# Hybrid decoder step: gate rows through DRAM, key norms on ScalarE, head steps one projection step earlier

## The reference, cut to what matters

```
q = l2_normalize(q) * DK_B ** -0.5 ; k = l2_normalize(k)       # over the 128 channels of a token
gcum = cumsum(g)                                               # over the tokens of a chunk
decay = where(tril, exp(gcum[:, None] - gcum[None, :]), 0)
lower = tril((k * beta) @ k.T * decay, -1)                     # solve (lower + I) u = ...
attn = (q @ k.T) * decay
kg = k * exp(gcum[-1] - gcum)
...
o = rms_norm(o, norm_g) * silu(z)
```

## Time and profile before

| | before |
|---|---|
| median of 3 runs | 2000.53 us (1999.17 to 2001.12) |
| the profiled execution: its own time, its span | 2001.81 us, 2000.0 us |
| PE busy, share of the span | 1962.6 us, 98% |
| DVE, ACT, POOL busy | 1234.6, 733.6, 670.3 us |
| chain that ended last, PE's share | 86% |

### The profile page before, as it was taken

How to read it: one execution, slowest core, us unless ns; L and a number is a source line. 1 busy time by engine, 2 the same in 40 slices (tenths; PEclk the granted TensorE clock), 3 DMA queues, 4 the chain that set the end, 5 groups by cost and what they waited for, 6 DMA issues and landing times.

```text
span 2000.0 us, 37378 instructions
## 1 busy us (share of the span) xinstructions
PE 1962.6 (98%) x15596; PEld 1902.4 (95%) x15596; DVE 1234.6 (62%) x2460; ACT 733.6 (37%) x1268; POOL 670.3 (34%) x659
## 2 busy tenths in 40 slices
PE   6999999999999999999999999999999999999997
PEld 4999999999999988889999999999999999999997
DVE  6666566756663435665433389999999954563334
ACT  5422222232222124544212255555555543352220
POOL 4123212311320222002211158888888840031110
PEclk9999999999999999999999999999999999999998
DMA  5221222112222234112344333333332322223333
GB/s 195 75 64 56 65 66 64 65 56 64 66 70 89 94 139 162 54 54 77 121 132 132 108 107 91 89 95 95 96 95 87 86 75 85 85 91 120 101 105 113
DMA packets 79721, 184.14 MB, mean 92 GB/s; under 512 B 26776, under 2 KB 35928, under 8 KB 79304
## 3 DMA queue, kind: packets, MB, share of 16 engines
q1 hardware_dynamic: 72304, 166.22, 27.2%
q0 software_dynamic: 3504, 9.63, 1.4%
q10 hardware_dynamic: 3744, 5.90, 0.8%
HBM read 162.66 MB, written 19.06 MB: 91 GB/s over the span
## 4 chain that ended last, share of the span: by engine, by line
PE 86%; DVE 10%; issue 1%; POOL 1%; ACT 1%; DMA 0%; SPq 0%; POOLq 0%; DVEq 0%; ACTq 0%
PE acc L580 71%; DVE arena L1551 2%; DVE full L1554 2%; PE acc L654 2%; DVE w_lo L1551 2%; PE gp L778 1%; DVE act_lo L1551 1%; PE acc L682 1%; POOL small L2295 1%; PE gp L788 1%; PE gp L884 1%; PE gp L770 1%; PE gp L936 1%; DVE full L1551 1%; PE gp L766 1%
## 5 line engine op out<-in xcount | busy, mean ns | idle before, releaser
L580 PE MATMUL acc<-act_hi,w_hi 128*128 128x288 f32 x3904 | 861.2, 302 | 0.3 <-DVE w_lo L1551 0.3
L580 PE MATMUL acc<-act_hi,w_lo 128*128 128x288 f32 x3904 | 836.4, 296 | 0.0
L580 PE MATMUL acc<-act_lo,w_hi 128*128 128x288 f32 x3904 | 835.4, 296 | 0.0
L580 PEld LDWEIGHTS acc<-act_hi,w_hi 128*128 128x128 f32 x3904 | 625.2, 189 | 14.7 <-issue 9.5
L580 PEld LDWEIGHTS acc<-act_hi,w_lo 128*128 128x128 f32 x3904 | 628.9, 189 | 0.0
L580 PEld LDWEIGHTS acc<-act_lo,w_hi 128*128 128x128 f32 x3904 | 627.9, 189 | 0.0
L2295 POOL TENSOR_TENSOR arena<-arena 128x512 f32<-128x512 f32 (+2 forms) x281 | 386.9, 1377 | 348.0 <-ACT arena L1397 284.1
L1093 ACT ACTIVATE w_hi<-w_raw 128x1024 fp32r<-128x1024 f32 x264 | 277.1, 1054 | 416.0 <-PE acc L580 309.9
L1551 DVE TENSOR_TENSOR w_lo<-w_raw,w_hi 128x1024 fp32r<-128x1024 f32 x264 | 382.4, 1468 | 41.3 <-ACT w_hi L1093 40.4
L1554 DVE SCALAR_TENSOR_TENSOR gp<-arena,par,gp 128x64 f32<-128x64 f32 (+1 forms) x688 | 248.0, 441 | 0.0
L1093 ACT ACTIVATE arena<-arena,par 128x512 f32<-128x512 f32 x240 | 165.1, 720 | 95.6 <-POOL arena L2295 88.0
(11 more groups left out here) (263 smaller groups left out, 1784.0 us busy)
## 6 DMA issues: line engine op xcount, KB each, us to landing
w_raw<-wt SPq DMA_DIRECT2D x264, 512.0 KB, 4.0
full<-x SPq DMA_DIRECT2D x16, 288.0 KB, 6.9
arena<-x SPq DMA_DIRECT2D x16, 288.0 KB, 3.7
arena<-x_scratch SPq DMA_DIRECT2D x16, 288.0 KB, 2.8
x_scratch<-full ACTq DMA_DIRECT2D x14, 288.0 KB, 3.9
out_y<-full SPq DMA_DIRECT2D x24, 144.0 KB, 1.9
arena<-state_in SPq DMA_DIRECT2D x6, 512.0 KB, 4.1
out_sdn<-arena POOLq DMA_DIRECT2D x6, 512.0 KB, 3.1
```

The costliest lines, as they stand in the source:

```text
L580: ins = pe.matmul(acc[:, s, i, 0:HALF], w[:, s, wk], a[:, k, i * HALF:(i + 1) * HALF], start=(k == 0 and j == 0), stop=(k == KT - 1 and j ...
```

## The change

What it does:

- The running sums of the gates of all heads come out of four more matmuls in `gate_sums`, once, with the 8 heads as output rows. DVE copies them to SBUF (`g_turned`), POOL stores them in DRAM (`g_dram`, 8 rows of 512), and for each head POOL loads one row into all 128 partitions (`gate_row`, `g_row`): for head 0 at step 30 of the unit before, for head `it + 1` at step 9 of the unit of head `it`. `gcum` and `gB` are gone; `dmask` reads `g_row` from SBUF and waits for that DMA.
- `sq` squares q alone. The squares of k are made by ACT from the transposed k in PSUM, four activations of 128 columns with a sum each (`ksq`), after `kv_tok`. `norm` has four matmuls in place of eight; `ssum` has two instructions and also waits for `ksq`.
- With `gcum` gone, `norm`, `gram` and all head steps behind them up to `so3`, with what the other engines do for them, stand one projection step earlier: `a3` at step 10, `so3` at step 28, `osq` and `f1` to `f5` at 29, `on` at 30. `o_chan` stays behind step 0. On DVE `kg` moves from step 1 to behind `attn`.

```
-PE_HEAD = (["kv_tok", "gcum", "norm", "gram"] + ...
+PE_HEAD = (["kv_tok", "norm", "gram"] + ...
-PE_PLAN = {1: "kv_tok", 2: "gcum", 3: "norm", 4: "gram"}
-PE_PLAN |= {11 + i: n for i, n in enumerate(PE_HEAD[4:-1])}
+PE_PLAN = {1: "kv_tok", 2: "norm", 3: "gram"}
+PE_PLAN |= {10 + i: n for i, n in enumerate(PE_HEAD[3:-1])}
-DVE_PLAN = {1: ["kg"], 2: ["dmask"], 3: ["ssum"], 4: ["vs", "Mt", "attn"], 6: ["mc", "solve", "Xt", "X"]}
+DVE_PLAN = {2: ["dmask", "ssum"], 3: ["vs", "Mt", "attn", "kg"], 5: ["mc", "solve", "Xt", "X"]}
-POOL_PLAN = {0: ["scalars", "gB"], 3: ["nrm", "rn", "bn", "bp"], 4: ["B"], 7: ["L3"], 8: ["L4"]}
+POOL_PLAN = {0: ["scalars"], 2: ["nrm", "rn", "bn", "bp"], 3: ["B"], 6: ["L3"], 7: ["L4"]}
...
                 pe.matmul(gp[:, 1, 80:144], ones[0:NS, :], gmask.rearrange("p h b -> p (h b)"), start=True, stop=True)
+                for c in range(NC):
+                    pe.matmul(gp[0:H, 2, c * P:(c + 1) * P], gates[:, :, KG, c], tri, start=True, stop=True)
...
-                elif name == "gcum":
-                    pe.wait_ge(pool_h.sem, pool_h.at("gB", it))
-                    for c in range(NC):
-                        ins = pe.matmul(gp[:, 2, ck(c)], gB[:, c, :], tri, start=True, stop=True)
                 elif name == "norm":
                     pe.wait_ge(act_h.sem, act_h.at("sq", it))
-                    for c in range(8):
-                        ins = pe.matmul(gp[:, 3, c:c + 1], sqkq_c[:, c, :], ones[:, 0:1], start=True, stop=True)
+                    for c in range(NC):
+                        ins = pe.matmul(gp[:, 3, c:c + 1], q_sq[:, ck(c)], ones[:, 0:1], start=True, stop=True)
...
+                elif name == "ksq":
+                    act.wait_ge(pe_h.sem, pe_h.at("kv_tok", it))
+                    for c in range(NC):
+                        ins = act.activation(k_sq[:, c, :], gp[:, 0, c * P:(c + 1) * P], ACT.Square,
+                                             accum_out=ksum[:, c:c + 1])
...
                 elif name == "dmask":
-                    pe_at("gcum")
-                    ins = tt(dec, bank4(2), per_group(negm, 4), ADD)
+                    dve.wait_ge(g_in, 16 * (it + 1))
+                    ins = tt(dec, g_row, per_group(negm, 4), ADD)
...
+            def gate_row(it):
+
+                row = g_dram[it].unsqueeze(0).to_broadcast([P, SEQ])
+                pool.dma_start(g_row, row.rearrange("p (c t) -> p c t", t=P)).then_inc(g_in, 16)
...
+                            if 8 * ti + e == 9 and it < H - 1:
+                                pool.wait_ge(dve_h.sem, dve_h.at("dmask", it))
+                                gate_row(it + 1)
+                        if hp == 0 and (ti, e) == (3, 2):
+                            pool.wait_ge(prep, 3)
+                            pool.dma_start(g_dram, g_turned).then_inc(g_stored, 16)
+                        if hp == 0 and (ti, e) == (3, 6):
+                            pool.wait_ge(g_stored, 16)
+                            gate_row(0)
```

More of the change, by code:

```diff
@@ L100 @@
 LV = range(FIRST, LEVELS)
-PE_HEAD = (["kv_tok", "gcum", "norm", "gram"] + [f"{s}{i}" for i in LV for s in ("a", "x")]
+PE_HEAD = (["kv_tok", "norm", "gram"] + [f"{s}{i}" for i in LV for s in ("a", "x")]
            + ["u0", "so0"] + [f"{s}{c}" for c in range(1, NC) for s in ("s", "u", "so")] + ["o_chan"])
@@ L104 @@
 assert LEVELS == 7
-DVE_HEAD = (["kg", "dmask", "ssum", "vs", "Mt", "attn", "mc", "solve", "Xt", "X"]
+DVE_HEAD = (["dmask", "ssum", "vs", "Mt", "attn", "kg", "mc", "solve", "Xt", "X"]
             + [n for i in LV for n in [f"X{i}"] + [f"T{i}"] * (i in IN_BLOCKS)]
@@ L108 @@
             + ["on", "y"])
-ACT_HEAD = ["sq", "decay"] + [f"A{i}" for i in LV] + [f"q{c}" for c in range(1, NC)] + ["osq"]
-POOL_HEAD = (["scalars", "gB", "nrm", "rn", "bn", "bp", "B"] + [f"L{i}" for i in LV]
+ACT_HEAD = ["sq", "ksq", "decay"] + [f"A{i}" for i in LV] + [f"q{c}" for c in range(1, NC)] + ["osq"]
+POOL_HEAD = (["scalars", "nrm", "rn", "bn", "bp", "B"] + [f"L{i}" for i in LV]
              + ["f1", "f2", "f3", "f4", "f5"])
-PE_PLAN = {1: "kv_tok", 2: "gcum", 3: "norm", 4: "gram"}
-PE_PLAN |= {11 + i: n for i, n in enumerate(PE_HEAD[4:-1])}
+PE_PLAN = {1: "kv_tok", 2: "norm", 3: "gram"}
+PE_PLAN |= {10 + i: n for i, n in enumerate(PE_HEAD[3:-1])}
 def counts(names):
@@ L145 @@
 PE_AT = {n: i for i, n in PE_PLAN.items()}
-ACT_PLAN = {1: ["sq"], 2: ["decay"]} | {PE_AT[f"a{i}"]: [f"A{i}"] for i in LV}
-ACT_PLAN |= {PE_AT[f"s{c}"]: [f"q{c}"] for c in range(1, NC)} | {30: ["osq"]}
-DVE_PLAN = {1: ["kg"], 2: ["dmask"], 3: ["ssum"], 4: ["vs", "Mt", "attn"], 6: ["mc", "solve", "Xt", "X"]}
+ACT_PLAN = {1: ["sq", "ksq"], 2: ["decay"]} | {PE_AT[f"a{i}"]: [f"A{i}"] for i in LV}
+ACT_PLAN |= {PE_AT[f"s{c}"]: [f"q{c}"] for c in range(1, NC)} | {29: ["osq"]}
+DVE_PLAN = {2: ["dmask", "ssum"], 3: ["vs", "Mt", "attn", "kg"], 5: ["mc", "solve", "Xt", "X"]}
 DVE_PLAN |= {PE_AT[f"x{i}"]: [f"X{i}"] + [f"T{i}"] * (i in IN_BLOCKS) for i in LV} | {PE_AT["u0"]: ["vp0"], PE_AT["so0"]: ["S0", "o0"]}
@@ L182 @@
 SATT_DVE = {5: "bias", 10: "prob", 14: "turned_new", 20: "out0", 26: "out1"}
-POOL_PLAN = {0: ["scalars", "gB"], 3: ["nrm", "rn", "bn", "bp"], 4: ["B"], 7: ["L3"], 8: ["L4"]}
-POOL_PLAN |= {PE_AT[f"a{l - 2}"] + 1: [f"L{l}"] for l in range(5, LEVELS)} | {30: ["f1", "f2", "f3", "f4", "f5"]}
+POOL_PLAN = {0: ["scalars"], 2: ["nrm", "rn", "bn", "bp"], 3: ["B"], 6: ["L3"], 7: ["L4"]}
+POOL_PLAN |= {PE_AT[f"a{l - 2}"] + 1: [f"L{l}"] for l in range(5, LEVELS)} | {29: ["f1", "f2", "f3", "f4", "f5"]}
 DVE_TAPS = 16
@@ L297, in hybrid_step @@
         diagonal = (lower, upper)
[L298 to L299 removed]
+        q_sq = fa[:, 3584:4096]
+        k_sq = fa[:, 4096:4608].rearrange("p (c t) -> p c t", t=P)
         o_sq = fa[:, 4096:4608].rearrange("p (c t) -> p c t", t=P)
@@ L1162, in head_act @@
                         act.wait_ge(pe_h.sem, pe_h.at("o_chan", it - 1))
-                    ins = act.activation(sqkq, kqv[kb][:, 0:2, :], ACT.Square)
+                    ins = act.activation(q_sq, kqv[kb][:, 1, :], ACT.Square)
+                elif name == "ksq":
[3 more added lines that the diff above has]
+                                             accum_out=ksum[:, c:c + 1])
                 elif name == "decay":
+                    act.wait_ge(pool_h.sem, pool_h.at("scalars", it))
                     act.wait_ge(dve_h.sem, dve_h.at("dmask", it))
@@ L1759, in head_dve @@
                 elif name == "dmask":
-                    pe_at("gcum")
-                    ins = tt(dec, bank4(2), per_group(negm, 4), ADD)
+                    dve.wait_ge(g_in, 16 * (it + 1))
+                    ins = tt(dec, g_row, per_group(negm, 4), ADD)
                 elif name == "ssum":
                     pe_at("norm")
-                    ins = ts(ssum, gp[:, 3, 0:8], EPS, None, ADD)
+                    dve.wait_ge(act_h.sem, act_h.at("ksq", it))
+                    ts(ssum[:, 0:4], ksum, EPS, None, ADD)
+                    ins = ts(ssum[:, 4:8], gp[:, 3, 0:4], EPS, None, ADD)
                 elif name == "vs":
@@ L2376, in head_pool @@
                     ins = copy(hs, gates[:, it])
-                elif name == "gB":
-                    own("scalars")
-                    ins = copy(gB, per_row(hs[:, KG, 0:4], P))
                 elif name == "nrm":
```

9 lines of the change are left out of this document (7 added, 2 removed).

## The result

The changed kernel takes 1978.76 us (median of four runs, 1975.62 to 1980.16), the kernel before on the same chip 2000.76 (1999.17 to 2001.12): a ratio of 0.989, 95% interval 0.9876 to 0.9904. Run again, unedited, beside other kernels, it took 1980.7 (before 1998.88) and 1980.9 (before 2000.69). The runs of one kernel scatter: those of before that stood beside these two went from 1991.99 to 2003.98. Over these three rounds the gain was 22.0, 18.2 and 19.8 us, and the two later medians lie inside the forecast's range of 1979 to 1989. So the times alone can't say where 3 us come from, and the rest of this text goes by the traces, where the heads' stretch of PE repeats to 0.1 us.

The account below looks back on a forecast made before the run. PE's chain of projection matmuls and head steps bounds the kernel; 12.95 us of work removed plus 5.6 of waits make 18.55, from 2001.81 to 1983.3, forecast as a median of 1982.0 us, range 1979 to 1989.

Parts of the forecast that it names:

- PE's work: Matmuls on PE's chain: gcum's 0.89 us and half of norm's 1.68 go, 13.84 us for eight heads, less added matmuls.
- The added matmuls: Four float32 matmuls added once in gate_sums, priced like gcum at 0.89 us, possibly nothing if hidden.
- PE's waits: PE standing still at o_chan and kv_tok: 0.80 us a head goes for seven heads, 5.6 us in all.
- The range: Total time from 1979 to 1989 us; its low end assumed free added matmuls, no last o_chan wait, less a3 wait.
- the 0.5 that was to be a sign of being wrong: At a3 in each head: the forecast is wrong if PE waits over 0.5 us there.
- `kv_tok`'s wait: PE's 0.28 us wait at kv_tok, behind y, silu and late on; goes because on comes 1.6 us early.
- `o_chan`'s wait: PE's 0.52 us wait at head's end goes: so3 a step earlier, S3 and o3 ahead of the split, 1.6 us spare.
- `kg` at nothing: DVE's added 0.69 us between attn and the split costs nothing, since POOL's B already holds up the split.
- The rival in which `kg` isn't covered: The split is released later by kg's length, a3 0.69 us later for eight heads: 1987.5 us, chance 0.13.
- The rival in which `L3` gets in first: The split, issued after POOL's L3 starts, waits 1.29 us more a head, 10.3 in all: 1992.3 us, chance 0.09.
- The gate row: POOL's row load: issue 0.65 to 2.6 us, landing up to 4; rival, issue holds up solve: 2002.8 us, chance 0.03.
- `ksq` ahead of `norm`: ACT's four squares of k take 1.4 us after kv_tok; norm ends 2.4 us after it, so ssum doesn't wait.

Follow-up runs that it names:

- norms_on_pe: Changed kernel with q and k both squared from SBUF on ACT and both norms summed by PE: 7.2 us more in the heads, median 5.8 above after_again.
- no_shift: Changed kernel with its work removed but every head step at its old projection step: 3.72 us more in the heads' stretch, 4.5 in the median.
- no_shift_spread: no_shift with POOL's spread of the gates put back into a free buffer: median 1985.35 us, 534.32 for the eight heads' matmuls.
- end_late: Changed kernel with only osq, f1 to f5 and on back at their old steps: median 1982.12 us, 528.39 for the eight heads' matmuls.
- kg_early: Changed kernel with kg moved to step 2, right behind ssum: 528.47 us for the eight heads' matmuls.
- kg_twice: Changed kernel with kg made twice in its place, first into a free buffer: median 1992.23 us, 538.24 for the eight heads' matmuls.
- after_again: Changed kernel, unedited, run again for a second profile: median 1980.7 us.
- before_again: Kernel before the change, unedited, run again for a second profile; its heads' stretch repeated to 0.06 us.

## Why the prediction was right in kind and 3.4 us short

Side, places and most of the mechanism came as forecast; the sum was too small, 18.55 us for 22.0. Of the 3.4 us the traces give 2.5 to the kernels (21.03) and 0.96 to scatter of the start, and another round gave 18.2 us in all: that the median came out below the range by 0.24 us is partly scatter. Of the 2.5, 1.69 are a fall of the clock that may have been missing by luck. Its steps:

- **PE's work: right, one term small.** `norm`'s half was priced at half of the row, 0.84; it is 1.68 - 0.78 = 0.90 by the chains, and 0.90 by norms_on_pe. The intervals between projection matmuls in which these steps stand shrank by 7.1 us at `norm` and 7.0 at `gcum` over the eight heads: 14.1, not 13.84. The added matmuls: 0.83, forecast 0.89.
- **PE's waits: this is the term that failed.** "I count 0.52 + 0.28 = 0.80 us for the seven heads that have a successor: 5.6 us, and leave out the last `o_chan`." What it left out is most of the miss: the last `o_chan` and the 192 projection matmuls behind it were put at nothing and gave 1.92 us, 0.23 for that wait and 1.69 for the granted clock that fell to 0.5 behind it in the kernel before. The fall at 649 us stood in the trace of before; whether the change is what took it away stays open. What the term did count came 0.6 too small: between projection matmuls the two places gave 1.19 - 0.62 = 0.57 and 1.36 - 1.06 = 0.30 at the head shown, and 3.9 and 2.2 over the seven heads, 6.2 us. A step that waited also takes longer from its own start to the next projection matmul (`o_chan` 0.41 against 0.36, `kv_tok` 0.82 against 0.79), which the starts ahead of it don't show. `a3` took 0.4 back. 14.1 + 6.2 - 0.4 = 19.9, what the heads' stretch shows.
- **The range: too narrow at its low end.** It was made of the added matmuls at nothing, the last `o_chan` and a part of `a3`'s wait; of these only 0.23 us came, and the clock, the small terms above and some 1 us of scatter at the start had no place in it. Of `a3` one head was read, "at most 0.32": head 0 waited 0.9 before and 1.0 now (1.26 less the 0.26 of a switch), over the 0.5 that was to be a sign of being wrong; it cost no more than the other heads' share, since it was late already.
- **Why `kv_tok`'s wait went: wrong cause.** "With `on` 1.6 us early, it goes too." It went with POOL's spread, `on` late or not (no_shift, no_shift_spread); the prediction names the spread as a hindrance of `silu` and gives it no price. Whether the earlier `on` would have been enough beside the spread was not tried. By the three kernels the 19.94 us are 548.38 - 534.32 = 14.06 for PE's work, 2.16 for the spread, 3.72 for the shift.
- **Why `o_chan`'s wait went: half right.** That `so3` comes a step earlier, with `S3` and `o3` ahead of the split, is what did it; the place of `osq` was argued with as much weight and carries none (end_late).
- **`kg` at nothing: right, for the reason given.** `L3` together with `B` is as long as before, the split is 1.34 and ends 3.6 us after `gram`, as forecast. The rival in which `kg` isn't covered falls with kg_early, where taking `kg` out gained nothing. The rival in which `L3` gets in first didn't happen, but its mechanism and price are real: 1.22 us a head in kg_twice against 1.29.
- **The gate row: right, but for what comes behind it.** POOL issues it in 0.62 us, the store in 1.33, and it lands in 3.7. For head 0 DVE waited 1.0 us for it, PE not at all. The issue doesn't hold up the solve on DVE: the first two products take 1.14 us, 1.15 before, beside `L4` in both (the last of it, now, beside the issue), and the next two 0.38, 0.37 before. But the third two take 0.45, 0.38 before. Beside them now run two small products of POOL (`arena<-arena,cst`, 0.40), which came before the second two in the kernel before and stand behind the issue and a wait for ACT now. POOL, then DVE:

```profile
305.40 0.62 POOL L2374 DMA_DIRECT2D full<-gate_rows  x1
306.57 0.40 POOL L2306 TENSOR_TENSOR arena<-arena,cst 128x3 f32<-128x3 f32 x2 [0.54 <-ACT arena L1095]
```

```profile
304.54 1.14 DVE L1559 TENSOR_TENSOR arena<-arena 128x4 f32<-128x4 f32 x2
...
305.93 0.38 DVE L1559 TENSOR_TENSOR arena<-arena 128x8 f32<-128x8 f32 x2
...
306.55 0.45 DVE L1559 TENSOR_TENSOR arena<-arena 128x12 f32<-128x12 f32 x2
```

  It is so in heads 0 to 6. Head 7 has no such products of POOL there, the third two take 0.38, and `a3` is 0.55 behind its pair, 0.57 before. That fits the 0.06 or so that `a3` lost in the others; no run has the shift without this meeting, so it isn't shown.

- **`ksq` ahead of `norm`: right.** Its last read of a sum starts at 360.57 and ends at 360.79, `norm` ends at 361.97.

From `gram` to `gram` a head takes 363.66 - 297.61 = 66.05 us; 66.1 was forecast.

## What to carry to other kernels

When a wait of the bound engine is to go, take its price from the last piece of work ahead of the step to the first one behind it, and walk the trace to its end: a fall of the clock behind the waits belongs into the range even if nothing says whether it will come again. When two things stand between a late event and a waiting step, one of them may hold the whole wait; the product on DVE that showed twice its usual length beside work on POOL was such a wait, and it went when that work went. And what is added on DVE right behind POOL's work may be free as long as it stays ahead of POOL's next product, and cost twice its length right after that: measure how much room is left (here one `kg` fits and two don't).

## What the runs showed that was not expected

**Matmuls at two paces.** In the same window of both kernels (us, busy times with counts, granted clock, DMA share, GB/s), before and then after:

```profile
947.00:1126.00 179.00, 179.00 (x1343) 178.80 (x1342) 66.63 (x51) 40.86 (x47) 27.39 (x18) 1.00 0.41 126
```

```profile
947.00:1126.00 179.00, 179.00 (x1378) 179.00 (x1377) 64.09 (x57) 41.82 (x55) 25.45 (x23) 1.00 0.40 125
```

PE has no idle time and a granted clock of 1.00 in both, and does 35 matmuls more in the second: 192 of them take 24.96 us there and 25.60 in the first. It isn't the change: after_again took 25.6 in that stretch, and before_again went over to 24.96 from about 1183 us until 1557, which put it 9.6 us ahead, until PE waited 7.6 us for another engine (its next matmul starts at 1590.58) and the granted clock fell to 0.5 for 6.83 us. The profiled execution of the changed kernel owes 4.2 us to this, and much of the scatter between runs may be of this kind. What sets the pace is open.

**A fall of the clock that comes or not.** At the sampled heads' norm the granted clock fell to 0.5 (1.2 GHz) for 3.41 us in both profiles of the kernel before and in one of the three with the late split, and in none of the nine others: not in the changed kernel's three, and not in no_shift_spread, whose waits ahead of that place are those of the kernel before. What the engine did just before was the same with and without a fall: 32 matmuls of one column. Seven of the fourteen profiles have a fall at another place, between 1561 and 1637 us, for 3.41 or 6.83 us, with the change and without it. What decides is open; at the sampled heads' norm it was worth 1.4 to 1.7 us each time.
